# Projection tiles for the retention moved between the steps of the prompt attention, half a tile at a time, in every second round

## The reference, cut to what matters

```python
def mixer_inputs(h, pos, lp):
    xn = rms_norm(h, lp['norm_mix'])
    rq, rk, rv, rg, qa, ckv, kr, gr, gm = split_cols(xn @ lp['w_in'])
    ...
def mla_prompt(q, c, kr, lp):          # 8 heads, 96 wide, causal softmax, 64 wide values
    k = mla_keys(c, kr, lp['w_uk'], lp['g_kn'])
    ...
    s = jnp.einsum('bqhd,bkhd->bhqk', qb, kk) * scale
    s = jnp.where(k_pos[None, :] <= q_pos[:, None], s, -jnp.inf)
    p = jax.nn.softmax(s, axis=-1)
    return jnp.einsum('bhqk,bkhd->bqhd', p, vv)
# reference(): for prompt and sample each
#   retention_chunk(rq, rk, rv, state, log_gamma)      4 heads, 128 wide keys, 256 wide values
#   mla_prompt(...) or mla_decode(... pages of the cache ...)
#   finish_layer: r = silu(rg) * rms_norm(o_ret) @ w_ret_o ; m = o_mla @ w_mla_o
#                 h + (sigmoid(gr)*r + sigmoid(gm)*m) @ w_out, then the squared-ReLU MLP
```

## Time and profile before

| | us |
|---|---|
| median of 3 runs (lowest, highest) | 1537.98 (1536.03, 1542.46) |
| the profiled execution, its own time | 1537.18 |
| its span | 1535.4 |
| TensorE busy, share of the span | 1447.3, 94% |
| VectorE, ScalarE, GpSimd busy | 776.4, 606.8, 295.4 |
| mean granted clock of TensorE, of full speed | 0.965 |

### The profile page before, as it was taken

How to read it: one execution, slowest core, us unless ns; L and a number is a source line. 1 busy time by engine, 2 the same in 40 slices (tenths; PEclk the granted TensorE clock), 3 DMA queues, 4 the chain that set the end, 5 groups by cost and what they waited for, 6 DMA issues and landing times.

```text
span 1535.4 us, 33521 instructions
## 1 busy us (share of the span) xinstructions
PE 1447.3 (94%) x11404; PEld 1358.9 (89%) x11404; DVE 776.4 (51%) x1450; ACT 606.8 (40%) x1503; POOL 295.4 (19%) x481
## 2 busy tenths in 40 slices
PE   7867987999999999999999999999999999999998
PEld 6755667999899899999998988889999999999998
DVE  6663553556456456555243553545465433344344
ACT  3443444656556556552123433432223421133211
POOL 3160003545445445540000000000040000000000
PEclk9987997999999999999999999999999999999999
DMA  5002106656455555542243233232222222222222
GB/s 219 17 0 58 40 18 193 183 147 176 145 149 176 146 148 176 159 135 97 83 138 101 98 124 103 73 127 84 95 87 77 96 83 96 95 84 96 89 104 82
DMA packets 118396, 168.70 MB, mean 110 GB/s; under 512 B 25393, under 2 KB 96082, under 8 KB 117458
## 3 DMA queue, kind: packets, MB, share of 16 engines
q1 hardware_dynamic: 118290, 167.30, 34.6%
HBM read 153.20 MB, written 7.47 MB: 105 GB/s over the span
## 4 chain that ended last, share of the span: by engine, by line
PE 70%; issue 6%; POOL 3%; DVE 2%; ACT 2%; DMA 1%; POOLq 0%; SPq 0%; DVEq 0%; ACTq 0%
PE ps L1319 37%; PE ps L1037 17%; PE ps L1477 8%; POOL ct_lo L745 2%; PE ps L1529 1%; PE ps L1061 1%; PE ps L1538 1%; PE ps L1518 1%; DMA ring_raw<-in_reto 1%; ACT o_tok L1628 1%; PE ps L1507 1%; PE ps L1521 0%; PE ps L1023 0%; PE ps L1051 0%; POOL kr_squares L762 0%
## 5 line engine op out<-in xcount | busy, mean ns | idle before, releaser
L1037 PE MATMUL ps<-wq_hi,ct_hi 128*128 128x260 f32 x1024 | 302.7, 296 | 8.9 <-POOL ct_lo L745 8.9
L1037 PE MATMUL ps<-wq_hi,ct_lo 128*128 128x260 f32 x1024 | 291.9, 285 | 0.0
L1037 PE MATMUL ps<-wq_lo,ct_hi 128*128 128x260 f32 x1024 | 291.8, 285 | 0.0
L896 DVE TENSOR_REDUCE k_sums<-k_squares 128x8 f32<-128x512 f32 (+1 forms) x256 | 175.3, 685 | 191.5 <-ACT k_squares L802 189.2
L745 POOL TENSOR_TENSOR ct_lo<-ct_raw,ct_hi 128x256 fp32r<-128x256 f32 x256 | 188.9, 738 | 346.4 <-ACT ct_hi L795 345.9
L802 ACT ACTIVATE k_squares<-ps 128x512 f32<-128x512 f32 x256 | 153.4, 599 | 183.2 <-PE ps L1037 178.8
L1216 ACT ACTIVATE ring_hi<-ring_raw 128x1024 fp32r<-128x1024 f32 x106 | 108.2, 1021 | 256.2 <-PE ps L1319 207.2
L1037 PEld LDWEIGHTS ps<-wq_hi,ct_hi 128*128 128x128 f32 x1024 | 195.3, 191 | 13.1 <-issue 11.7
L1037 PEld LDWEIGHTS ps<-wq_lo,ct_hi 128*128 128x128 f32 x1024 | 195.4, 191 | 0.0
L1037 PEld LDWEIGHTS ps<-wq_hi,ct_lo 128*128 128x128 f32 x1024 | 195.1, 191 | 0.0
L1319 PE MATMUL ps<-x_hi,ring_hi 128*128 128x260 f32 (+1 forms) x768 | 156.4, 285 | 0.0
(11 more groups left out here) (302 smaller groups left out, 2697.6 us busy)
## 6 DMA issues: line engine op xcount, KB each, us to landing
ct_raw<-in_ct SPq DMA_DIRECT2D x256, 144.0 KB, 2.2
c_values<-in_c SPq DMA_DIRECT2D x256, 128.0 KB, 2.4
ring_raw<-in_wmain SPq DMA_DIRECT2D x40, 512.0 KB, 3.5
ring_raw<-in_up SPq DMA_DIRECT2D x32, 512.0 KB, 3.4
ring_raw<-in_down SPq DMA_DIRECT2D x32, 512.0 KB, 3.6
state_new<-in_state SPq DMA_DIRECT2D x4, 1024.0 KB, 5.3
out_st_s<-state_new SPq DMA_DIRECT2D x4, 1024.0 KB, 4.4
ring_raw<-in_reto SPq DMA_DIRECT2D x8, 512.0 KB, 3.5
```

The source lines that it names most:

```text
L896: dve.tensor_reduce(to, k2[:, j].rearrange("p b h d -> p (b h) d"), AX.X, ALU.add).then_inc(red_done, 1)
L1037: mm = nc.tensor.matmul(k_ps[j % 2][:, f, 0:WQN], ch[:, j, r * P:(r + 1) * P], of_sequence(w, b)[:, r, f, :], start=(r == 0 and x == 0), s ...
```

## The change

The 16 projection tiles of the retention leave their own stage and are worked on inside the prompt attention, which is written anew as 51 rounds (`PromptAttention`). A head takes six rounds: queries turned, keys turned, then four tiles of 128 query tokens with all keys up to them (144, 272, 400, 528). Round i does the step i on TensorE, then its piece of the projection, then the values of step i-3, then the turning of step i-2. A piece is half a tile, 24 products in one go, in 26 of the 51 rounds (3, 5, 7, 9, 10, 12, 14, ... 24, 26, 27, 29, ... 39, 41, 42, 44, ... 50), and nothing in the others; the last six halves follow behind the rounds, with the set-up of the decode part between them. ScalarE and VectorE split the next tile in the round that follows a finished one. The results go through a staging buffer to DRAM (`z_scratch`) and come back head by head in the gate stage.

Besides: the heads are read straight from `q_tok`, `k_tok` and `v_tok`, without DMAs; the meta tokens' own queries are left out; the mask is added by a rounded product; the probabilities are turned unscaled and the outputs scaled instead (L726), with 64 columns per value product instead of 128; the outputs are turned back at the end. In the gate stage the heads start at slots 6, 15, 24 and 33 instead of 0, 11, 22 and 33, and the closing of the last sequence lies in slots 0 to 8.

```diff
+def eighths_after(i):
+    if i < FIRST_FILL:
+        return 0
+    n = i - FIRST_FILL + 1
+    return min((2 * n + (n + EXTRA - 1) // EXTRA) // 4 * 4, 8 * 16 - 4 * TAIL_HALVES)
...
+    def evacuate(self, dve, half):
...
+        self.nc.vector.tensor_tensor(self.staged[:, g % 4, at], self.ps[3][:, b, 0:HT], m.rx[:, at], ALU.mult).then_inc(self.half_out, 1)
+    def eighth(self, pe, n):
...
+        if quarter == 0:
+            pe.wait_ge(ring.lo_done, g + 1)
+            wait(pe, self.half_out, half - 1)
+        for k in (2 * quarter, 2 * quarter + 1):
+            for j, (w, x) in enumerate(((ring.hi[s], m.xh), (ring.hi[s], m.xl), (ring.lo[s], m.xh))):
+                mm = nc.tensor.matmul(self.ps[3][:, b, 0:HT], w[:, k, :], x[:, k, b * HT:(b + 1) * HT],
...
+        def turn(h, t):                       # tensor
+            u = NQ * h + t
+            pe.wait_ge(self.exp_done, u + 1)
+            wait(pe, self.pt_out, 2 * u)
+            wait(pe, self.pv_out, u)
...
+        for i in range(ROUNDS):               # tensor
+            parts = list(range(eighths_after(i - 1), eighths_after(i)))
...
+            for n in parts:
+                self.eighth(pe, n)
+            h, t = self.step(i - LAG_VALUES)
+            if h is not None and t >= 0:
+                values(h, t)
+            h, t = self.step(i - LAG_TURN)
+            if h is not None and t >= 0:
+                turn(h, t)
...
+        def exp(i, h, t):                     # scalar
+            u, end = NQ * h + t, N_META + (t + 1) * P
+            act.wait_ge(self.max_done, u + 1)
+            wait(act, self.pt_done, u - 1)
...
+            for half in self.halves_between(eighths_after(i - 2), eighths_after(i - 1)):
+                if half % 2:
+                    self.split_hi(act, half // 2 + 2)
+            if h is not None and t >= 0:
+                exp(i, h, t)
+            h, t = self.step(i - LAG_TURN)
+            if h is not None and t >= 0:
+                take_turned(h, t)
...
+        for i in range(ROUNDS):               # vector
+            for half in self.halves_between(eighths_after(i - 2), eighths_after(i - 1)):
+                self.evacuate(dve, half)
+                if half % 2:
+                    self.split_lo(dve, half // 2 + 2)
+            h, t = self.step(i)
+            if t == -1:
+                keys(i, h)
+            elif h is not None and t >= 0:
+                maximum(i, h, t)
...
+            h, t = self.step(i - 1)
+            if h is not None and t >= 0:
+                invert(h, t)
+            h, t = self.step(i - LAG_VALUES)
+            if h is not None and t >= 0:
+                take_values(h, t)
...
+    def load_head(self, sp, h):
+        sp.dma_start(self.m.z[:, 4 * h:4 * h + 4, :], self.d_z[:, 4 * h:4 * h + 4, :]).then_inc(self.z_in, 16)
+        sp.wait_ge(self.z_in, 16 * h + 16)
...
+                if slot == 10:                # SP, in the gate stage
+                    sp.wait_ge(o_out, 1)
+                    for h in range(1, RH):
+                        rest.load_head(sp, h)
...
+            pe.wait_ge(rope_free, NGR * NB)
+            pe.wait_ge(k_free, NPG * NB)
+            rest.tensor(pe, close)
```

More of the change, by code:

```diff
@@ L692, in _ @@
             sp.dma_start(ukr[:], m.d_uk).then_inc(set_in, 16)
-            for s in range(2):
-                sp.dma_start(ring.raw[s][:], m.d_wmain[s]).then_inc(ring.loaded[s], 16)
             sp.wait_ge(set_in, 48)
@@ L715, in sequence @@
                     pages = table_row(NGR * b + g)
[L716 to L717 removed]
+                    keys(NGR * b + g, g % 2, pages)
                     if g == 0:
[L719 to L727 removed]
+                        sp.wait_ge(cv_in, 16 * NPG * b)
+                        sp.wait_ge(pv_done, 1 * b)
+                        new_row(b, x2)
+                    values(x2, g, pages)
+            for g in range(2):
+                keys(g, g % 2, table_row(g), first=True)
+            att.sync(sp)
+            sp.wait_ge(att.pv_out, NQ * MH)
+            for g in range(2):
+                values(0, g, table_row(g))
+            for g in range(14, 16):
+                att.store(sp, g)
+            rest.fetch(sp, 0)
+            rest.fetch(sp, 1)
+            sp.wait_ge(crow_set, 1)
+            new_row(0, 0)
+            for g in range(2, NGR):
+                pages = table_row(g)
+                keys(g, g % 2, pages)
+                values(0, g, pages)
+            sp.wait_ge(att.ot_turned, NQ)
+            for n in range(4):
+                sp.wait_ge(att.stored[n], 64)
             with sp.Fori(0, NB // 2 - 1) as twice:
@@ L1580, in tensor @@
-        self.after.tensor(pe, (self.xr_done, 2 * RH))
-    def scalar(self, act):
+            close(slot)
+            for h in range(RH):
+                r = slot - FIRST_HEAD - HEAD * h
+                if r == 11:
+                    turn_back(h)
+                if r in (2, 3, 4):
+                    turn(h, 2 * r - 4)
+                    turn(h, 2 * r - 3)
+                if r == 5:
+                    scores(h, 0)
+                    scores(h, 1)
+                    scores(h, 2)
+                if r == 6:
+                    scores(h, 3)
+                    scores(h, 4)
+                    outputs(h, 0)
+                    outputs(h, 1)
+                if r == 7:
+                    outputs(h, 2)
+                    outputs(h, 3)
+                    outputs(h, 4)
+                    new_states(h)
+                if r == 8:
+                    new_outputs(h)
@@ L2041, in program @@
         project_tokens(nc, m, ps)
-    chain = project_retention(nc, m, ps, ring)
-    with nc.cleanup_on_exit():
-        prompt_attention(nc, m, ps)
-    chain.count()
+    z = nc.dram_tensor("z_scratch", [P, 4 * RH, T], F32, kind="Internal").ap()
     finish = Chain(nc, ps, ring, [], ahead=True)
-    heads = GatedRetention(nc, m, ps, ring, chain, finish)
+    heads = GatedRetention(nc, m, ps, ring, z, finish)
     m.gate_done, m.ret_lo = heads.gate_done, heads.xr_lo
@@ L2052, in program @@
     finish.stages += stages + more
-    decode_attention(nc, m, ps, ring, chain, heads)
+    decode_attention(nc, m, ps, ring, PromptAttention(nc, m, ps, ring, z), heads)
     return m
```

735 lines of the change are left out of this document (391 added, 344 removed).

## The result

The changed kernel took 1568.24 us (median of 4 runs, 1566.35 to 1570.24), the kernel before 1538.3 us beside it: a ratio of 1.0194, 95% interval 1.0169 to 1.0219. The forecast was 1544 with a range up to 1562, so it was wrong in size, and its likeliest case was not the one that came. The profiled execution took 1566.4 us with a span of 1564.6.

What follows compares the result with a forecast made beforehand. TensorE's work and stalls bound the kernel. Rounds of 205 us and a 24.8 tail start the pages 100.6 later; the projection stage gives 102.7; with smaller terms, +6.7 on 1537.2 gives 1543.9 us, range 1521 to 1562 (8 in 10).

Steps and rivals of the forecast that it cites:

- likeliest case: Whole kernel: stalls as walked, the rounds take back what the removed stage gives; 1544 us, 1532 to 1556; chance 0.38.
- The walk of the waits: TensorE's stalls in the rounds: outputs 12.5 us, probabilities some 5, splits 15.5 in seven rounds.
- The wait ahead of the gates: Between pages and gates: the gates now wait for the last page's sums, +2.0 us.
- The work: TensorE's work in the 51 rounds: 77 us for eight heads and 77 for 26 half tiles, together 154.
- The clock: In the rounds: seven gaps of 2.7 to 3.2 us lower TensorE's clock, 1.4 us each, together 10.
- the start: Start of the rounds: 5.5 us for the first half tile's weights and split, 2.5 for 1.2 GHz, together 8.
- the faster case: In the rounds: the new form saves its work and the stalls hide; rounds of 182, 1521 us; chance 0.30.
- the slower rival: In the rounds: paid splits and unfilled rounds hold 1.2 GHz, some 16 us of work doubles; 1560 us; chance 0.22.
- the tail: Behind the rounds, up to the first page: six halves, absorbed products, output turnings and a wait, together 24.8 us.
- transfer: Gate stage: head loads delay ring fetches, each stopping TensorE about 5 us, twice at most; 1552 us; chance 0.10.
- The closing: The last sequence's closing moves from the projection stage into gate slots, so 7.8 us come back.

Runs made afterwards that it cites:

- the attention by itself: Changed kernel with nothing dealt into the attention's rounds, the 26 half tiles following as a stage of their own: 1592.4 us, ratio 1.0354.

## Why the prediction was wrong

**The walk of the waits was right but for one.** Seven long waits in rounds 6, 13, 17, 25, 36, 43 and 47, none in 10, 21, 28, 32 and 40; seventeen short ones of 0.54 (0.52 forecast); 33.4 us in all. That the total fits is in part luck: six of the long ones were 0.3 to 0.6 us shorter than the 2.7 walked, and the one of round 6 was 2.1 longer, since its weights came late behind the page fetches. The wait ahead of the gates was 1.7 instead of 2.0. The work was 159 us instead of 154. The scores' own prices add up to 3.4 us per head, not 3.2, which is 1.4 of these five; in the rest, busy times include the instructions' pipelines, which differences of starts leave out.

**The step that failed is "The clock".** It counted seven falls of 1.4 us, 10 in all, and the start 2.5 for the same cause: 12.5. Measured, TensorE was busy for 59.7 us at 1.2 GHz, which cost some 30 by the comparison under the table. These 17.4 us too little are as large as the whole miss of the rounds; the work (+4.6) and the start's standing (-5.5) nearly cancel. Three readings were wrong. The row it went by, 0.56 for 3.4 us behind a wait of 2.80, stands between pages, where TensorE then has nothing but dense products; in the rounds most low stretches were 6.8 us long (one was 10.2, two were 3.4), and they stretched the scores and the next half tile with them. Waits of 2.08 stood beside a fall each time, where the faster case had room for gaps just under 2.8 to pass. And unfilled rounds without a long wait fell as well, which the slower rival named and the forecast left out. The forecast read one row of the clock as a price per wait; it is a state of the whole neighbourhood.

**The slower rival was the case.** Its mechanism (low through the following round, and unfilled rounds too) is what the traces show. It counted 16 us more than the forecast for work at half speed; there were 17.4. That it gave 1560 and not 1566 is the rest of the table of stages: the gates' 4, the tail's 1.5 and the first turning's 1.1, less 1.4 in the pages and behind the gates. I gave it 0.22, since the window from 154 to 156 before stayed at 1.00 with 1.25 of 2.0 us busy. That window was too short a witness: it lay among rounds that are 85 to 98% busy at the full clock. The start was the other way about: its 5.5 us of standing were 1.4 of waits, the rest was work that I had counted twice.

**Gates, +4.** No transfer was late there. The heads at nine slots instead of eleven put a head's results (1.24 us on ScalarE) ahead of the next one's tokens, 2 x 1.8 us; I had given the closer spacing nothing. The run that moved them took 3.3 of the 3.6 away. The closing brought a wait of 2.3 us for `max_diag` (L1271) into the gates, which the projection stage before does not have. Together these are 5.9 us of idle time, against 1.8 counted (0.8 of the 7.8 moved, and 1 for a fetch). The clock has no part in it: it was low for 23.9 us in the gates before and after.

**Left open.** Which property of the work the clock follows is not settled here: not the share of time in which TensorE is busy by the profile (11.21 of 12 us at 0.50, 12.71 of 15 at 1.00), and not whether the instructions are turnings or products (the pair that filled the waits). Three low stretches of the changed kernel (154, 256, 331 us) were not taken away one by one. Whether the attention before keeps its clock by its denser order alone wasn't tried.

## What to carry to other kernels

Work that is dealt into a latency-bound stage pays by how evenly it is dealt, not only by how much: the same products took 1568 us in pieces of 2.96 us in every second round and 1524 us in pieces of 1.5 us in every round. Price a wait on TensorE as its length and the slow stretch behind it, read the clock in windows of half a microsecond in a place with the same density, and where it is low, try added, useless products: if the kernel gets faster, the clock was the cost. Then let each instruction wait only for what it touches: the one to four turnings that write another bank needn't wait for the outputs, and that alone was worth 29 us in this kernel (the clock's share in it included).

## What the runs showed of the hardware

In the changed kernel, low stretches in the rounds were 3.4 us (from 154.0), 6.8 (from 174.5) and 10.2 (from 137.0). TensorE can be busy by the profile for 93% of a stretch and stay at 1.2 GHz (11.21 of 12 us, in the attention by itself). Work at 1.2 GHz cost about half of its busy time (23.1 us for 47.1). Added products of 268 columns between the same small instructions raised the granted clock of the attention from 0.55 to 0.95. Transposes in the long waits kept the clock as well as products did (41.6 and 45.1 us low, against 73.2 with neither). With 13 us of products ahead of a barrier the clock held over the barrier's 2.7 us and fell at 119.5, 1.3 us behind it. A stage that no edit touched also differs between profiles: the gates had 20.5 to 30.7 us at 1.2 GHz and took 240.5 to 246.7 us.
